# A hybrid diffusion transformer: x's sum between filter transforms, diagonals ahead of values, a fourth unit with its own bank

## What is computed

```python
h = modulate(rmsnorm(x, g[0]), mod[0], mod[1])        # shift, scale from silu(c) @ ada_w
y = mixer(h)                                          # layer 0 attention, layer 1 Hyena
x = x + mod[2] * rmsnorm(y, g[1])
h = modulate(rmsnorm(x, g[2]), mod[3], mod[4])
x = x + mod[5] * rmsnorm(square(relu(h @ w1)) @ w2, g[3])
# filters: sin, sin, a matmul, times a decay window, then a Fourier transform of each
```

## Time and profile before

| | us |
|---|---|
| median of 3 runs | 1448.31 |
| lowest, highest run | 1447.42, 1449.3 |
| the profiled execution, its own time | 1449.06 |
| its span, first to last instruction | 1447.3 |
| TensorE busy / weight load busy | 1377.5 / 1133.5 |
| VectorE, ScalarE, GpSimd busy | 899.7, 617.2, 122.9 |
| mean granted TensorE clock | 0.983 |

### The profile page before, as it was taken

How to read it: one execution, slowest core, us unless ns; L and a number is a source line. 1 busy time by engine, 2 the same in 40 slices (tenths; PEclk the granted TensorE clock), 3 DMA queues, 4 the chain that set the end, 5 groups by cost and what they waited for, 6 DMA issues and landing times. The chain is left out here.

```text
span 1447.3 us, 18140 instructions
## 1 busy us (share of the span) xinstructions
PE 1377.5 (95%) x6672; PEld 1133.5 (78%) x6672; DVE 899.7 (62%) x1291; ACT 617.2 (43%) x919; POOL 122.9 (8%) x149
## 2 busy tenths in 40 slices
PE   8989999999999999999998998898999999999996
PEld 2568788988878888888877787787887888888885
DVE  6878769977665555554466999988363333333333
ACT  3645446664362433415445434424445233252441
POOL 1761120002000000000100000000100000000011
PEclk9999999999999999999999999999999999999998
DMA  9535251119166565655212222230312323223221
GB/s 366 197 131 176 83 164 44 45 60 331 46 204 203 185 205 185 199 193 166 89 71 73 78 83 73 88 103 29 117 44 87 102 88 102 87 101 101 87 87 58
DMA packets 48265, 178.48 MB, mean 123 GB/s; under 512 B 5863, under 2 KB 6183, under 8 KB 45768
## 3 DMA queue, kind: packets, MB, share of 16 engines
q1 hardware_dynamic: 45192, 164.51, 33.4%
q0 software_dynamic: 3008, 13.11, 2.8%
HBM read 164.49 MB, written 10.49 MB: 121 GB/s over the span
## 5 line engine op out<-in xcount | busy, mean ns | idle before, releaser
L1727 PE MATMUL bank<-hhi,whi 128*128 128x512 f32 (+1 forms) x936 | 353.0, 377 | 9.3 <-ACT scratch L973 5.6
L1729 PE MATMUL bank<-hhi,wlo 128*128 128x512 f32 (+1 forms) x936 | 350.2, 374 | 0.0
L1728 PE MATMUL bank<-hlo,whi 128*128 128x512 f32 (+1 forms) x936 | 350.1, 374 | 0.0
L686 ACT ACTIVATE whi<-raw 128x1024 fp32r<-128x1024 f32 x180 | 189.5, 1054 | 216.2 <-PE bank L1729 199.4
L1109 DVE TENSOR_TENSOR wlo<-raw,whi 128x1024 fp32r<-128x1024 f32 x180 | 222.1, 1234 | 94.6 <-ACT whi L686 93.4
L1727 PE MATMUL bank<-ghi,whi 128*128 128x512 f32 x576 | 224.3, 389 | 4.7 <-DVE glo L1652 2.8
L1729 PE MATMUL bank<-ghi,wlo 128*128 128x512 f32 x576 | 224.1, 389 | 0.0
L1728 PE MATMUL bank<-glo,whi 128*128 128x512 f32 x576 | 224.1, 389 | 0.0
L1727 PEld LDWEIGHTS bank<-hhi,whi 128*128 128x128 f32 x936 | 177.0, 189 | 41.3 <-ACT whi L686 10.0
L1729 PEld LDWEIGHTS bank<-hhi,wlo 128*128 128x128 f32 x936 | 177.0, 189 | 31.4
L1728 PEld LDWEIGHTS bank<-hlo,whi 128*128 128x128 f32 x936 | 177.1, 189 | 30.8
(11 more groups left out here) (272 smaller groups left out, 2009.9 us busy)
## 6 DMA issues: line engine op xcount, KB each, us to landing
raw<-in_wpack SPq DMA_DIRECT2D x180, 512.0 KB, 3.5
araw<-in_apack SPq DMA_DIRECT2D x40, 512.0 KB, 3.6
amore<-in_apack SPq DMA_DIRECT2D x36, 512.0 KB, 3.5
ablk<-in_ahead SPq DMA_DIRECT2D x8, 1024.0 KB, 11.0
spectra<-scratch SPq DMA_DIRECT2D x16, 512.0 KB, 3.2
araw<-spectra POOLq DMA_DIRECT2D x8, 1024.0 KB, 5.0
fs<-in_fw SPq DMA_DIRECT2D x2, 1024.0 KB, 11.2
x<-in_xT SPq DMA_DIRECT2D x1, 2048.0 KB, 11.9
```

What stands on the lines that cost most here:

```text
L686: A(whi[:, s, :], raw[:, r, :], ACT.Copy).then_inc(hi_done, 1)
L1727: mm(o, lh, rh, start=first, stop=False)
L1728: mm(o, lh, rl, start=False, stop=False)
L1729: return mm(o, ll, rh, start=False, stop=last)
```

## The change

1. *Head.* VectorE clears `tap2[:, 0]`, and TensorE runs two 128x512 matmuls on it into `B3` before it waits for the first load.
2. *x's sum.* The matmul over x's squares stands between transforms 2 and 3, no longer inside transform 4; the squares' root follows on ScalarE before tile 10's high parts. Tile 11 stands between the halves of transform 3 and tile 14 between those of transform 4. The reciprocal is four pieces of 128x128 (`x_inverse`), each between other steps of VectorE. Filter output (0, 0) comes ahead of weight sums 3, the weight preparations 0 and 1 come behind filter outputs 2 and tile 13.
3. *Attention.* The `rq` reciprocal and the eight diagonals stand ahead of `values_lo(0)`, and ScalarE's two copies of `crow` one step later, behind the second exponential.
4. *Boundaries.* TensorE sums the first four chunks of half 1 before `x_rows(b, 0)`; ScalarE's root for half 0 comes behind two squares of half 1. The fourth unit has the bank `B2` and waits for no evacuation that is not long done; the fifth and sixth wait for `evac_done` of the first and second.

The banks:

```diff
-        FIRST_BANKS = (AB[:, 0, :], AB[:, 1, :], SC[:, 0, :])
+        FIRST_BANKS = (AB[:, 0, :], AB[:, 1, :], SC[:, 0, :], B2[:, :])
```

On ScalarE:

```diff
+            filter_odd(0, 0)
             weight_his(2)
-            filter_odd(0, 0)
+            filter_odd(0, 1)
             weight_his(3)
-            filter_odd(0, 1)
...
-            act.wait_ge(w3_lo, 4)
-            prep(0, 0, 0)
             filter_odds(1)
             x_square(2)
             x_square(3)
-            prep(1, 1, 1)
             filter_his(8)
             filter_his(9)
             filter_odds(2)
+            act.wait_ge(w3_lo, 4)
+            prep(0, 0, 0)
+            act.wait_ge(eps_set, 1)
+            act.wait_ge(xss_done, 1)
+            A(S[:, 9, :], B2[:, :], ACT.Sqrt, scale=1.0 / D, bias=epst[:, 0:1]).then_inc(sd_done, 1)
             filter_his(10)
...
                 if n == 1:
                     values_hi(1)
+                if n == 2:
                     act.wait_ge(csum_done, 1)
...
                     for i in range(4):
+                        if h and i == 2:
+                            x_root(b, 0)
...
-                    if h == 0:
-                        x_root(b, 0)
```

On VectorE:

```diff
+            nc.vector.memset(tap2[:, 0, :], 0.0).then_inc(warm_set, 1)
...
+            def x_inverse(i):
+                dve.wait_ge(sd_done, 1)
+                part = S[:, 9, i * P:(i + 1) * P]
+                nc.vector.reciprocal(part, part).then_inc(rs_done, 1)
...
             filter_outs(2)
+            prep(0, 0, 0)
             filter_tile(10)
+            x_inverse(0)
+            filter_out(3, 0)
             filter_tile(11)
-            filter_outs(3)
+            x_inverse(1)
+            filter_out(3, 1)
             filter_tile(12)
             filter_tile(13)
-            filter_outs(4)
+            prep(1, 1, 1)
+            filter_out(4, 0)
             filter_tile(14)
+            x_inverse(2)
+            filter_out(4, 1)
             filter_tile(15)
-            inverse_root(0, S[:, 9, :], NT)
+            x_inverse(3)
+            dve.wait_ge(rs_done, 4)
             filter_out(5, 0)
```

On TensorE:

```diff
+            pe.wait_ge(warm_set, 1)
+            for i in range(2):
+                mm(B3[:, :], tap2[:, 0, 0:P], tap2[:, 0, :], start=True, stop=True)
...
-                    if i == 30:
+                    if i == 22:
                         pe.wait_ge(sd_done, 1)
...
+            pe.wait_ge(gen_used, 19)
+            pe.wait_ge(xadd_done, 4)
+            mm(B2[:, :], ones, XSQ[0][:, 0, :], start=True, stop=True).then_inc(xss_done, 1)
...
                 x_sums(b, 0)
+                x_sums(b, 1, range(4))
                 x_rows(b, 0)
-                x_sums(b, 1)
+                x_sums(b, 1, range(4, KC))
...
+            def fourth_unit(u0):
+                unit(u0 + 3, 3, FIRST_BANKS[3], hhi, hlo, evacs=u0).then_inc(unit_done, 1)
```

81 lines of the change are left out of this document (45 added, 36 removed).

## The result

| | before | after |
|---|---|---|
| median | 1447.87 us (1446.80 to 1449.30, 4 runs) | 1429.76 us (1428.98 to 1430.65, 4 runs) |
| ratio after to before | | 0.9876 (95% interval 0.9864 to 0.9888) |
| span of the profiled execution | 1447.3 us | 1428.5 us |
| TensorE busy | 1377.5 us | 1373.1 us |
| mean granted clock | 0.983 | 0.988 |

A forecast was written before the change was run, and what follows sets the result against it. TensorE, busy 1377.5 of 1447.3 us, was taken as the bound, so gains come from its waits and half-clock matmuls. Terms 1.1 + 5.9 + 2.4 + 4.7 + 0.7 + 6.1 = 20.9 off 1449.06, less 0.75, gave 1427.4 us (1421 to 1435).

The forecast's parts named there:

- the marks named: Signs expected in the profile after, at the head, transform 6, `vlo`, the fourth unit's evacuation, boundary 1's taps and the clock.
- Part 1, the head: Start of kernel: warm-up matmuls may bring the clock up before the first block; gain 1.1 us (0 to 2.2).
- 3.5 instead of 6.2: Head: the sign that the first block's eight records take 3.5 us, where they took 6.2.
- Part 2, filters and x's sum: Filter transforms: the new order lets transform 6 start at 100.0, not 105.90; gain 5.9 us (3 to 8).
- Part 3, attention's entry: Attention's start: diagonals hidden in a wait, scores 2 start 1.8 us earlier, plus 0.6 of clock; gain 2.4 (1.7 to 3.3).
- Part 4, boundary 0: Boundary 0: split sum 1.9 us and fourth unit's missing evacuation wait 2.8; gain 4.7 (3.2 to 5.2).
- Boundary 1: Boundary 1: sum gains 1.9 us, own bank 0, half clock behind longer taps wait costs 1.2; gain 0.7 (-0.5 to 4.2).
- another stretch falls to 0.50 in exchange: Anywhere: a new half-clock stretch costs 3.0 us; part of a rival at 1431.5 us, chance 0.15.
- Boundary 2: Boundary 2: sum 0.3 us, missing evacuation wait 2.8, half clock behind it gone 3.0; gain 6.1 (2.8 to 6.4).
- The rival by which GpSimd holds x's sum: Filter stretch: GpSimd and VectorE shut each other out, gain there 3 us, not 5.9; 1430.3 us, chance 0.14.

The follow-up runs named there:

- e8: Changed kernel with x's second sum whole behind the wait for x's first root, as before the change: 1435.01 us.
- e10: Changed kernel with ten matmuls of no use ahead of Hyena's output units, in the earlier wait for weights: 1430.13 us.
- e11: Changed kernel with the edits of e9 and e10, plus matmuls of no use in the waits ahead of Hyena's inverse transforms and for boundary 1's taps: 1421.39 us.
- e3: Changed kernel with the old order of the filter stretch and the reciprocal whole; warm-up, attention and boundaries stay changed: 1433.73 us.
- e4: Changed kernel with x's reciprocal whole (128x512) where its last quarter stands: 1431.42 us.
- e5: Changed kernel with the diagonals and small reciprocal behind the first value parts again, and the conditioning copies in step 1: 1431.23 us.
- e6: Changed kernel with the fourth unit's own bank taken away at all three boundaries (old bank rotation): 1437.17 us.
- e7: Changed kernel with the fourth unit's own bank taken away at boundary 1 alone: 1429.41 us.
- e9: Changed kernel with the fourth Hyena unit's evacuation and taps at boundary 1 ahead of the weight preparation that waits for its load: 1426.40 us.
- e13: e12 with the boundaries' keep-busy matmuls back in place and the first two output units' weight preparations moved: 1419.51 us.
- e12: e11 without the ten matmuls, output chunks reordered, eight matmuls of no use before transform 4, boundary keep-busy matmuls between the sums' groups: 1418.42 us.

## Why the prediction was right, and where it was off

The sign and the time came as forecast, and so did, of the marks named, the missing waits at boundaries 0 and 2, the clock after boundary 2, the missing 2 us for `vlo`, and the waits for taps with half clock behind them. Two sizes were off: the first block (5.32, not 3.5), and transform 6, at 100.38 instead of 105.90, 5.5 earlier and not 7. The steps' misses, by the ledger from -1.0 to +0.5, add to 4.2 us without their signs and to 2.1 with them. Much of them is clock, which falls differently in each execution, so that they cancel in part is luck. One reading of the rows was wrong: that after most of TensorE's waits the next matmuls run at the lower level. In the profile before, behind the head, TensorE waited 1 us or more 21 times, and the clock fell in the wait or within 2.5 us behind it nine times. By its own steps:

- **Part 1, the head (1.1; measured 0.5 in the profile, 0.3 in the medians).** The middle between "comes up" and "does not" was a fair choice, but not for the reason given. Both happen, from one execution to the next: eight profiles had most of what the forecast priced at 2.2 (tile 0 at 22.2 to 22.5, 1.8 to 2.1 earlier than before), four had 0.4 to 0.5. The Trainium skill ("TensorE: Matmul & The Clock Gate", section "Part 1: The HAM clock gate") says that the moment at which the clock comes up is not tied to the kernel's start and differs from run to run; these twelve profiles agree. The mark "3.5 instead of 6.2" is thus seen in e8, e10 and e11 and not in the profile after.
- **Part 2, filters and x's sum (5.9; measured 5.3).** The mechanism is shown: e3 brings all three waits back, and VectorE's idle time over the stretch fell from 9.2 us in seven gaps to 3.5 in six (3.5 forecast). By e3 and e4, 1.8 is the pieces', 2.5 the rest of the order, and 0.9 the clock's. The pieces took 0.94 each (0.95 forecast). The wait before x's sum was 0.98, not 1.8: GpSimd's three large additions took 2.42 to 2.66, and all four with their gaps 9.8 (62.23 to 72.00), where the forecast had 10.5 from 3.21 each (three of that and a half make 11.2, so its sum was off as well); transform 4 then waited 1.95 for its low parts instead of 1.4, with 0.4 of half clock behind it.
- **Part 3, attention's entry (2.4; measured 2.6).** 1.7 for the diagonals by e5 (1.8 forecast) and 0.9 for the clock (0.6).
- **Part 4, boundary 0 (4.7; measured 5.2).** 2.0 for the sums, 3.1 for the bank, 0.1 ahead of them. e8 shows that all but 0.3 of the first is the clock's doing, as the working had it with its eight matmuls at half clock, and that it is no fixed 2.0: in another execution with the same wait the sums' part was 0.3.
- **Boundary 1 (0.7; measured -0.25).** That the bank gains nothing here, and why, is shown three times: e6, e7 and e9. The sum's 1.9 came in full (11.73 to 9.71, 2.0). What failed is a term that was not there: in the profile after the clock fell on the root's rows ahead of the sums (stretch at 724.0), which before had run at full clock, and that cost 1.0 (9.22 us from the first keep-busy to the sums; 8.23 before, and 8.23 in e4, where it did not fall either). The wait for taps was 2.81 with 1.13 ahead of it, 3.9 in all, as forecast (4.0), and the 1.3 behind it as forecast (1.2).
- **Between boundaries 1 and 2 (0; measured -1.0).** The one step that was missing. The wait of 2.8 inside the first output unit stood in both kernels, but the clock fell behind it only in the one after (1000.4). From that wait to the first keep-busy it took 43.21 us, 41.66 before: 1.55 lost. The three stages ahead of it had given 0.6. It fell there in all ten profiles of the changed kernel and its variants but e11 to e13, and not in e11, with a wait of 2.60; what decides it is open. The rival "another stretch falls to 0.50 in exchange" named this, and it came along with the forecast, not in its place. It was priced at 3.0 and cost 1.55 here and 1.0 at boundary 1.
- **Boundary 2 (6.1; measured 6.5).** As forecast: no wait, 1.00 behind it, 3.1 of clock and 0.2 for the sums. 0.3 more came ahead of the sums, where a stretch had fallen before (1059.9) and none did now, which the forecast did not have. e6 gives 4.7 for the bank in another execution, where one short stretch followed the wait.

**GpSimd and VectorE.** The rival by which GpSimd holds x's sum gave 1430.3, and the time came out beside it, but not by its way: that part gave 5.3, not 3. The rule under it is right. What the rows showed (a VectorE operation with its inputs in SBUF that meets a GpSimd operation stands until that ends, and the other way round) is what the Trainium skill states ("SBUF — State Buffer", section "SBUF: two separate sides"): whoever is first has the shared ports for the whole instruction. The prediction took it for a loss of 1.0 a step against "up to a whole addition", and the truth is between: a step loses what is left of the one operation that it meets, less some 0.13 (0.92, 0.85 and 2.23 were left here, 0.78, 0.72 and 2.09 were lost), and the moved preparations cost 2.00 and 1.94 where 2.24 was taken.

What the sum did not say plainly is that about a third of the gain is the clock's and not the order's. This is my estimate from the timelines: waits and work make 0.3 (head), 4.3 (filters), 1.7 (attention), 3.1 (boundary 0), 0.3 (boundary 1) and 3.1 (boundary 2), 12.8 in all; the other 6.0 us are half-clock stretches that fell elsewhere or not at all. Between the head and the end they take 41 us of the profile before and 27 of the one after. They change from execution to execution. In e6's six executions the time goes with the mean granted clock (1435.3 and 1435.4 us at 0.989, 1438.0 to 1441.0 at 0.985), but in the changed kernel's four it does not (1428.98 us at 0.986, 1430.65 at 0.987), so the clock is not all of the spread.

## What to carry to other kernels

Price a wait of TensorE as its length plus a chance of about 1.3 to 1.9 us for the matmuls behind it at half clock, and then ask whether those matmuls are the bound. Where TensorE sets the pace (the units behind the boundaries) they cost in full; where VectorE and GpSimd set it they cost little (0.4 at transform 4). An own bank gains only if the evacuation's engine is free to use it; look at what stands ahead of the evacuation in that engine's order, above all a step that waits for a load (e9 got 3.4 us by exchanging two steps). When an accumulation waits for its operands one by one, take them in the order in which they come (e12), and matmuls of no use can fill a wait that can't be shortened, but only in the very wait (e10 filled the one before), and only where something is to be had: they paid in Hyena's three waits of 3.6 us, and gave nothing at transform 4 and in the waits for taps that e9 had already shortened.

## What the runs showed of the hardware

- Fourteen 128x512 matmuls of no use (3.45 us) kept the clock up through each of Hyena's waits of 3.6 us. With them and e9's exchange the mean granted clock rose from 0.988 to 0.993 (e11).
- The same two f32 matmuls from 1.47 us on, 3.51 to 3.79 us long, were followed by full clock at 4.6 to 6.2 us in eight executions and by half clock until 14.0 to 14.3 in four.
- Of the half-clock stretches between the head and the end, all but two in fourteen profiles lasted 3.4 us, however long the wait ahead of them; the two of 6.8 stood in the kernel before (1094.0) and in e5 (768.6, behind the waits for taps), where it cost that execution 1.8 us.
- Behind the one-column sums of a boundary (16 records, 1.95 us), where TensorE hardly waited, the clock fell in ten of fourteen profiles at boundary 0 and in ten at boundary 1. In the changed kernel's it fell 0.4 us behind them. Three full matmuls put between their two groups (e12) did not prevent it in the one execution profiled.
- A reciprocal took 3.34 us for 128x512 and 0.94 for 128x128.
- A VectorE operation with its inputs in SBUF and a GpSimd operation did not run side by side: a weight preparation of 1.22 us took 2.00 and 1.94, a GpSimd subtraction of 1.29 took 2.28.
